# Second block's mixer rewritten: token-major queries and keys, twelve softmax units between recurrence levels and projections, eight bias transfers issued at once

## The chip, the core and the metric

The kernel runs on one NeuronCore of a Trainium2 chip. TensorE (PE) multiplies, VectorE (DVE) and ScalarE (ACT) work elementwise, GpSimd (POOL) issues some DMAs, SyncE (SP) issues the rest, and 16 DMA engines carry the data. Each engine runs its own list of instructions in order; semaphores tie the lists together. The metric is the device time of one execution in microseconds (us); less is better.

## The reference, cut to what is computed

256 tokens of width 1024 in fp32 pass through two equal hybrid layers (convolution, pooling and windowed attention with a distance bias, then a gated feed-forward part) and then through one other layer, the second block. The change is almost wholly in that block's mixer:

```python
h = rmsnorm(x, norm1_g) * (1 + sc1) + sh1                      # sc1, sh1 from c through w_ada
hq, hf, hi, hgt, nq, kc, vc, ks, vs, kw, vw, ng = split(h @ w_in)   # 4 x 512, 512, 6 x 128, 24 columns
# recurrence: 4 heads of 128, forget gate from hf
logf = log(lb + (1 - lb) * sigmoid(hf)); k = (1 - lb) * sigmoid(-hf); q = silu(hq); v = hi
S_t = exp(logf_t) * S_(t-1) + k_t v_t;  o_t = q_t S_t          # in all 256 tokens
o_hg = rmsnorm(o, norm_g) * silu(hgt)
# sparse attention: 8 query heads of 64, 2 key/value heads, first 16 dims of a head rotated
q, k_c, k_s, k_w = rope(rmsnorm(...) * gain)
k_cmp, v_cmp = silu((blocks of 32 tokens, stride 16, + pe) @ w1) @ w2       # 15 blocks
o_cmp = softmax(q k_cmp, masked) v_cmp
o_slc = softmax(q k_s over chosen blocks, causal) v_s          # 16 may be chosen, there are 4: all
o_win = softmax(q k_w, window 512, causal) v_w                 # the window is longer than the text
o_nsa = sigmoid(ng)[0] * o_cmp + sigmoid(ng)[1] * o_slc + sigmoid(ng)[2] * o_win
x = x + gt1 * (concat(o_hg, o_nsa) @ w_out)
x = x + gt2 * (feed-forward with a short causal convolution)
```

## The kernel before, in words

**Products.** Every fp32 value is held as two parts that fp32r can multiply: ACT makes the high one (L941), DVE the low one (L1237), and a product of the kernel is three matmuls (`product`, L587, L588, L589). Weights come as chunks of 1 MB through a ring of four slots on SP's queue. A chunk is split in two halves by ACT and DVE; chunk c+2 is split once the job that reads chunk c is over. Chunks of the compression weights (`c1k`, `c1v`) stay unsplit and are read as plain fp32.

**Jobs.** A job reads one chunk. `project` gives results with output columns on the partitions and 256 tokens in the free dimension: 48 products with 256 moving columns. `project_rows` gives them with tokens on the partitions: half of the contraction against 512 columns, 24 products with 512 moving columns, and two such jobs fill two banks. `project_tokens` is the same for up to 256 columns. Jobs 0 to 14 of the second block are `hf`, `hq`, `nq` (two each), `kc`, `ks`, `kw`, `vc`, `vv`, `ng` (the 24 branch gates, weights from the parameters), `hi`, `hg` (two each), and behind them four `out` jobs and the feed-forward part (`fa`, `fv`, `down`). `kc`, `ks`, `kw`, `vc` carry each head's columns twice, so that both halves of the partitions hold them.

**The recurrence.** It is computed as a 256 x 256 matrix of decayed products of queries and keys, by doubling levels: 0, then block sizes 1 to 64 (`LEVELS`), and a last one that joins the halves, nine in all. A level on PE is `level` (L761, 16 matmuls of 128 x 128, fp32, the last 8); DVE prepares its operands (`level_operands`, L1539 to L1550) between two exponentials on ACT (`level_exps`, L1086 to L1093) and copies its result out under a mask (`level_read_`, L1514, L1517). A table `HG_AT` puts levels behind certain jobs between `hq` 1 and `hi` 1.

**Behind the projections**, once the last level is read, stand one after the other: output of the recurrence (L776 to L778), mean squares of queries and keys and of the recurrence by matmuls with small picking tables (L783), their spreading over partitions (L799), a rotation matrix (L807), hidden layer of the compression (L823: each weight load is 30 columns of gathered blocks `Z`, and 256 weight columns move, 64 records in the trace for keys and values), its turning (L830), second weights (L837, L841), and eight softmax units: a unit is a pair of heads and half of the tokens, with two attention branches of up to 256 keys per head and the compressed one of 15. A unit goes scores (L860, L864) - `softmax2_in` on DVE (masked reads L1230, maximum) - exponentials on ACT (L1163) - `softmax2_out` on DVE (reciprocal, gates, scaling) - transposes (`turn2`, L876, L878) - copies on ACT (L1185, L1186) - values (L889 to L893). Then the four `out` jobs.

**The bias table.** At the program's start POOL writes the bias by distance to DRAM (L530) and reads it back skewed in eight transfers of 384 KB, two in flight: from the third on each waits for the one two before it (`bias_in`, L536). DVE's first masked read of the first layer's attention (L1230) waits for all eight.

## Time and profile before

| | us |
|---|---|
| median of 3 runs (1529.12 to 1537.22) | 1531.45 |
| the profiled execution, whole | 1538.83 |
| its span in the trace | 1537.0 |
| PE busy | 1430.1 |
| DVE busy | 1038.5 |
| ACT busy | 721.2 |
| POOL busy | 36.1 |
| mean granted clock of PE, share of full | 0.952 |

All numbers below come from the one profiled execution; its span begins with the first instruction and ends with the last. A busy PE need not be a PE at full speed: matmuls overlap, and the granted clock (PEclk) changes in the course of the span. A line number is that of kernel.py of the version shown (L587); "split", "h", "feed", "arena" and "psum" are names of tiles, where "h" is the normed input of the projections and "feed" the concatenated output of the mixer.

### The profile page before, as it was taken

The numbers are of one execution on the slowest core, as the hardware profiler recorded it, in microseconds if no ns is written. First come the engines' busy times: TensorE is split into PE (matmuls) and PEld (weight loads), VectorE is DVE, ScalarE is ACT, GpSimd is POOL, SyncE is SP. The second block draws the span as 40 slices with busy tenths as digits, with TensorE's granted clock in tenths as the row PEclk, the third lists the DMA queues.
The fourth block names the chain that finished last, engine by engine and source line by source line (L and its number), as shares of the span: only waits on it lengthen the run. The fifth ranks groups of instructions, "written<-read, shape, count | busy, mean of one in ns | idle before, by whom it ended". The sixth has DMA issues, their size and how long they took to land.

```text
span 1537.0 us, 25011 instructions
## 1 busy us (share of the span) xinstructions
PE 1430.1 (93%) x10188; PEld 1312.7 (85%) x10188; DVE 1038.5 (68%) x1679; ACT 721.2 (47%) x1128; POOL 36.1 (2%) x69
## 2 busy tenths in 40 slices
PE   7789998999999989999999999997999868899996
PEld 7679997988999989999989899996899445789995
DVE  4287677677677655876867767767665663677776
ACT  5244657444333444466563543335644163544452
POOL 0000000000000000000000000000000000000000
PEclk9889999999999999999999999998998876999998
DMA  9954544466767744544434576773442040445550
GB/s 273 208 183 155 175 165 138 145 203 216 254 230 256 252 145 140 169 161 162 140 133 169 204 259 240 246 258 117 141 165 86 4 161 1 135 170 175 192 192 28
DMA packets 41999, 262.98 MB, mean 171 GB/s; under 512 B 5195, under 2 KB 5451, under 8 KB 14372
## 3 DMA queue, kind: packets, MB, share of 16 engines
q1 hardware_dynamic: 32976, 229.66, 44.7%
q0 software_dynamic: 8784, 31.60, 6.1%
q8 instruction: 80, 1.31, 0.3%
q10 hardware_dynamic: 132, 0.18, 0.0%
q14 instruction: 27, 0.22, 0.0%
HBM read 259.85 MB, written 1.58 MB: 170 GB/s over the span
## 4 chain that ended last, share of the span: by engine, by line
PE 78%; DVE 11%; ACT 5%; DMA 5%; issue 2%; ACTq 0%; SPq 0%; POOL 0%; DVEq 0%
PE psum L587 23%; PE psum L588 23%; PE psum L589 23%; DMA arena<-bias_by_distance 4%; DVE split L1237 3%; DVE arena L1230 1%; ACT split L941 1%; PE psum L581 1%; PE psum L823 1%; PE psum L761 1%; PE psum L697 1%; PE psum L674 1%; DVE arena L1379 1%; PE psum L687 1%; ACT arena L958 1%
## 5 line engine op out<-in xcount | busy, mean ns | idle before, releaser
L587 PE MATMUL psum<-h,split 128*128 128x256 f32 x2304 | 662.3, 287 | 13.6 <-DVE split L1237 11.6
L588 PE MATMUL psum<-h,split 128*128 128x256 f32 x2304 | 656.3, 285 | 0.0
L589 PE MATMUL psum<-h,split 128*128 128x256 f32 x2304 | 656.0, 285 | 0.0
L1237 DVE TENSOR_TENSOR split<-ring,split 128x1024 fp32r<-128x1024 f32 x424 | 499.9, 1220 | 226.9 <-ACT split L941 226.2
L941 ACT CAST split<-ring 128x1024 fp32r<-128x1024 f32 x424 | 422.9, 1048 | 267.8 <-PE psum L589 255.6
L587 PEld LDWEIGHTS psum<-h,split 128*128 128x128 f32 x2304 | 446.5, 194 | 28.4 <-issue 16.7
L588 PEld LDWEIGHTS psum<-h,split 128*128 128x128 f32 x2304 | 446.8, 194 | 1.0
L589 PEld LDWEIGHTS psum<-h,split 128*128 128x128 f32 x2304 | 446.4, 194 | 0.0
L587 PE MATMUL psum<-split,feed 128*128 128x512 f32 x296 | 117.6, 397 | 5.6 <-DVE feed L1237 4.1
L588 PE MATMUL psum<-split,feed 128*128 128x512 f32 x296 | 117.1, 396 | 0.0
L589 PE MATMUL psum<-split,feed 128*128 128x512 f32 x296 | 116.5, 393 | 0.0
L587 PE MATMUL psum<-feed,split 128*128 128x256 f32 x288 | 84.0, 292 | 0.0
L589 PE MATMUL psum<-feed,split 128*128 128x256 f32 x288 | 82.5, 287 | 0.0
L588 PE MATMUL psum<-feed,split 128*128 128x256 f32 x288 | 82.5, 287 | 0.0
L1004 ACT ACTIVATE arena<-arena,small 128x256 f32<-128x256 f32 x64 | 32.1, 502 | 106.0 <-DVE small L1319 106.0
L1039 ACT ACTIVATE sig<-psum 128x512 f32<-128x512 f32 x46 | 27.5, 597 | 110.1 <-PE psum L589 110.0
L587 PEld LDWEIGHTS psum<-split,feed 128*128 128x128 f32 x296 | 56.7, 192 | 17.7 <-DVE feed L1237 4.6
L589 PEld LDWEIGHTS psum<-split,feed 128*128 128x128 f32 x296 | 56.6, 191 | 12.1
L588 PEld LDWEIGHTS psum<-split,feed 128*128 128x128 f32 x296 | 56.7, 192 | 10.7
L587 PEld LDWEIGHTS psum<-feed,split 128*128 128x128 f32 x288 | 56.4, 196 | 3.4 <-issue 3.4
L1451 DVE SCALAR_TENSOR_TENSOR arena<-arena 128x1024 f32<-128x1024 f32 x48 | 58.4, 1218 | 0.0
L588 PEld LDWEIGHTS psum<-feed,split 128*128 128x128 f32 x288 | 56.3, 196 | 0.0
(247 smaller groups left out, 1482.1 us busy)
## 6 DMA issues: line engine op xcount, KB each, us to landing
ring<-stream SPq DMA_DIRECT2D x215, 1024.0 KB, 4.9
arena<-ada POOLq DMA_DIRECT2D x48, 512.0 KB, 5.2
arena<-bias_by_distance POOLq DMA_DIRECT2D x8, 384.0 KB, 13.5
x<-x_in SPq DMA_DIRECT2D x2, 512.0 KB, 4.5
ring<-stream SPq DMA_DIRECT2D x2, 512.0 KB, 7.7
gain<-mod_rows POOLq DMA_DIRECT2D x2, 512.0 KB, 4.1
out<-x SPq DMA_DIRECT2D x4, 256.0 KB, 2.0
bias_by_distance<-arena POOLq DMA_DIRECT2D x1, 512.0 KB, 8.9
```

Source lines behind the costliest of these rows:

```text
L581: mm = pe.transpose(bank[(b0 + kt) % 8][:, i * P:(i + 1) * P], xs[:, i, kt * P:(kt + 1) * P], ident)
L587: pe.matmul(out_, a[0], b[0], start=first, stop=False)
L588: pe.matmul(out_, a[0], b[1], start=False, stop=False)
L589: return pe.matmul(out_, a[1], b[0], start=False, stop=last)
L674: mm = pe.matmul(bank[4 + hh][:, 0:T], qT[hh * HD:(hh + 1) * HD, p, n * P:(n + 1) * P], kd[hh * HD:(hh + 1) * HD, p // 2, :], start=True, ...
L687: mm = pe.transpose(bank[6][:, (2 * hh + s) * P:(2 * hh + s + 1) * P], S1[:, i % 2, hh, s * P:(s + 1) * P], ident)
L697: mm = pe.matmul(bank[7][hh * HD:(hh + 1) * HD, 0:T], v1[:, s, p // 2 * HD:(p // 2 + 1) * HD], PT[:, hh, s, :], start=(s == 0), stop=(s == 1))
L941: act.copy(split[:, c % 2, 0, n], ring[:, c % RING, n]).then_inc(wh_ready, 1)
L1004: act.activation(S1[:, i % 2, hh, :], S1[:, i % 2, hh, :], ACT.Exp, bias=nm[:, i % 2, hh:hh + 1], accum_out=rs[:, i % 2, hh:hh + 1])
L1039: act.activation(sig[:, i % 4], src, ACT.Sigmoid) \
L1237: return dve.tensor_tensor(out_, value, high.bitcast(F32), ALU.subtract)
L1451: dve.scalar_tensor_tensor(w, w, 1.0, c_row, ALU.mult, ALU.mult, accum_out=mod_l[:, a:a + 1]) \
```

## The change

Line numbers of after differ: L587 to L589 are L612 to L614, L761 is L786, L1237 is L1356, L1230 is L1349.

- **Order of chunks and jobs.** `nq`, `kk` (new: the two compression, selection and window keys and the compression values in one token-major job pair) come first, by rows; then `hf`, `hq`, `vv`, `ng`; the compression weights `c1k`, `c1v` come ahead of `hi` and `hg`, which are now by rows, too. `kc`, `ks`, `kw`, `vc` are gone: 13 projection chunks in place of 15. `out` is read in the order of quarters 0, 2, 1, 3: first both column halves of the recurrence's rows, last those of the attention's.
- **Norm and rotation token-major.** Squares on ACT (two), sums and root per token and head, scaling from PSUM on DVE; the rotation multiplies only the 16 rotated dims with tables that hold the gains (`rows_in`). Then 20 transposes (`turn_q`, `turn_k`) and copies on ACT with a gain per partition (`g_cols`). The picking, spreading and rotation matmuls and their tables are gone.
- **Hidden layer turned.** The weights are loaded, 128 columns at a time, and the 30 gathered blocks move: 128 records of 30 columns in place of 64 of 256, with no transposes behind them.
- **Compressed softmax once**, for all heads and tokens, in a few DVE instructions and one exponential.
- **Twelve units of 512 columns** (`unit2`): the first half of the tokens in units of two head pairs with 128 keys, the second half with one and 256 keys. `step(u)` issues scores of u+2, values of u-1 and transposes of u, and the steps stand between levels, `hg`, the recurrence's output and the `out` jobs.
- **The recurrence's output** is token-major, too, and is normed on DVE and transposed (`turn_hg`). The gate is kept token-major.
- **Zeroing** of six tiles goes to GpSimd, once the block's first norm has its input (`zeroed`); before, DVE zeroed two.
- **Bias.** The eight transfers are issued without waits between, on one semaphore.

```diff
@@ jobs and chunks
-    [("hf", 0), ("hf", 1), ("hq", 0), ("hq", 1), ("nq", 0), ("nq", 1),
-     ("kc", 0), ("ks", 0), ("kw", 0), ("vc", 0), ("vv", 0),
-     ("hi", 0), ("hi", 1), ("hg", 0), ("hg", 1)]
+    [("nq", 0), ("nq", 1), ("kk", 0), ("kk", 1), ("hf", 0), ("hf", 1), ("hq", 0), ("hq", 1), ("vv", 0)]
     + [("c1k", 0), ("c1k", 1), ("c1v", 0), ("c1v", 1)]
+    + [("hi", 0), ("hi", 1), ("hg", 0), ("hg", 1)]
     + [("out", j) for j in range(4)]
-HG_AT = {BJ["hq", 1] + a: i for i, a in enumerate((0, 1, 3, 4, 5, 7, 8, 10, 11))}
@@ POOL
-            for i, q0 in enumerate(range(0, P, SHIFTS)):
-                if i >= 2:
-                    pool.wait_ge(bias_in[i % 2], 16 * (i // 2))
+            for q0 in range(0, P, SHIFTS):
...
+            pool.wait_ge(x_ready, 8 * L + 4)
+            for a in (AT, hkh, SC, hid4, V4, kcmp):
+                pool.memset(a, 0.0).then_inc(zeroed, 1)
@@ PE, the order
+            h_in = each_of(h_ready, L * 16)
+            rows("nq", 0, h, 0, (0, 1), h_in)
+            rows("nq", 1, h, 1, (0, 1), h_in)
+            rows("kk", 0, h, 0, (2, 3))
+            rows("kk", 1, h, 1, (2, 3))
+            columns_of("hf", 0, 4)
+            turn_q()
+            columns_of("hf", 1, 5)
+            columns_of("hq", 0, 7)
+            turn_k()
...
+            level(0)
+            hidden(0)
+            level(1)
+            hidden(1)
+            level(2)
...
+            second_weights()
+            level(3)
+            score_compressed()
+            pe.wait_ge(*release2(("ng", 0)))
+            rows("hi", 0, h, 0, (4, 5))
+            scores2(0)
+            scores2(1)
+            rows("hi", 1, h, 1, (4, 5))
+            level(4)
+            turn_compressed()
+            pe.wait_ge(*release2(("hi", 1)))
+            rows("hg", 0, h, 0, (4, 5))
+            step(0)
+            level(5)
+            rows("hg", 1, h, 1, (4, 5))
+            step(1)
+            level(6)
+            step(2)
+            level(7)
+            step(3)
+            level(8)
+            hg_output()
+            step(4)
+            step(5)
+            pe.wait_ge(hg_read, 1)
+            turn_hg()
+            step(6)
+            pe.wait_ge(hmix_ready, 2)
+            rows("out", 0, feed, 0, (4, 5))
+            step(7)
+            rows("out", 1, feed, 0, (6, 7))
+            for u in range(8, UNITS2):
+                step(u)
+            values2(UNITS2 - 1)
+            mixed = {4 + 2 * p: (mix_ready, p + 1) for p in range(2)}
+            rows("out", 2, feed, 1, (4, 5), mixed)
+            rows("out", 3, feed, 1, (6, 7))
@@ new functions
+            def step(u):
+                if u + 2 < UNITS2:
+                    scores2(u + 2)
+                if u >= 1:
+                    values2(u - 1)
+                turn2(u)
...
+            def softmax2_out(u):
+                n, hh, ps = unit2(u)
+                groups = 2 * len(ps)
+                width = 4 * P // groups
+                dve.wait_ge(exp2, u + 1)
...
+                for g in range(groups):
+                    a = S2[u % 2][:, g * width:(g + 1) * width]
+                    ins = dve.tensor_scalar(a, a, rec[:, g:g + 1], None, ALU.mult)
                 ins.then_inc(p2_ready, 1)
@@ ACT, from level 5's exponentials on
+            level_exps(5)
+            split_high(15, L)
+            act.wait_ge(cmp_in, 1)
+            act.activation(cmp_p, cmp_p, ACT.Exp).then_inc(cmp_exp, 1)
+            exps2(0)
+            job_wait("hi", 1)
+            for i in range(NT):
+                e = act.copy(hv[:, i, :], bank[4 + i])
+            e.then_inc(act_evac, 1)
+            split_high(16, L)
+            exps2(1)
+            level_exps(6)
+            act.wait_ge(cmp_turned, 1)
```

PE, where the recurrence begins. Before, behind the product of the last job ahead of it (`hq` 1), level 0 and then a projection:

```order
L589 MATMUL psum<-h,split 128x256
L761 MATMUL psum<-arena 128x128 [waits hops_ready]
L761 MATMUL psum<-arena 128x128 x7
L587 MATMUL psum<-h,split 128x256 [waits wl_ready,act_evac]
L588 MATMUL psum<-h,split 128x256
L589 MATMUL psum<-h,split 128x256
```

After, behind `vv`, levels 0 and 1 with the hidden layer of the compression (L825; "ring" is the unsplit weight) between them:

```order
L614 MATMUL psum<-split,h 128x256
L786 MATMUL psum<-arena 128x128 [waits hops_ready]
L786 MATMUL psum<-arena 128x128 x7
L825 MATMUL psum<-arena,ring 128x30 [waits w_loaded1,z_ready]
L825 MATMUL psum<-arena,ring 128x30 x7
L825 MATMUL psum<-arena,ring 128x30 [waits w_loaded2]
L825 MATMUL psum<-arena,ring 128x30 x23
L786 MATMUL psum<-arena 128x128 [waits level_read,hops_ready]
L786 MATMUL psum<-arena 128x128 x7
L825 MATMUL psum<-arena,ring 128x30 [waits w_loaded3,z_ready]
```

The first levels had whole projections between them; now they have 64 small fp32 products each, with 30 moving columns.

DVE, the last levels of the recurrence before. L1514 and L1517 are the masked read and the copy of a level's result, L1237 the low half of a weight chunk, the others operands of a level:

```order
L1544 TENSOR_TENSOR arena<-arena 128x8x64 [waits hexp_q,level_done]
L1548 TENSOR_TENSOR arena<-arena 128x8x64 [waits hdiff]
L1550 TENSOR_TENSOR arena<-arena 128x8x64 [waits hexp_k]
L1514 COPY_PREDICATED arena<-pair_mask,psum 128x1024 [waits level_done,hcum_ready,hops_ready]
L1237 TENSOR_TENSOR split<-ring,split 128x1024 [waits wh_ready] x2
L1539 TENSOR_TENSOR arena<-arena 128x4x128
L1544 TENSOR_TENSOR arena<-arena 128x4x128 [waits hexp_q,level_done]
L1550 TENSOR_TENSOR arena<-arena 128x4x128 [waits hexp_k]
L1514 COPY_PREDICATED arena<-pair_mask,psum 128x1024 [waits level_done,hops_ready]
```

After, between the operands of one level and the read of the level before it stand a unit's scaling (L1771 to L1777) and the next unit's masked read and maximum (L1349, L1762, L1763):

```order
L1651 TENSOR_TENSOR arena<-arena 128x16x32
L1656 TENSOR_TENSOR arena<-arena 128x16x32 [waits hexp_q,level_done]
L1660 TENSOR_TENSOR arena<-arena 128x16x32 [waits hdiff]
L1662 TENSOR_TENSOR arena<-arena 128x16x32 [waits hexp_k]
L1771 RECIPROCAL arena<-arena 128x4 [waits exp2,hcum_ready,hops_ready]
L1774 TENSOR_TENSOR arena<-arena 128x4 [waits dve_step]
L1777 TENSOR_SCALAR sig<-sig,arena 128x128 [waits dve_step]
L1777 TENSOR_SCALAR sig<-sig,arena 128x128 x3
L1349 SCALAR_TENSOR_TENSOR sig<-psum,cst 128x512 [waits pt2_done,s2_done]
L1762 TENSOR_REDUCE arena<-sig 128x2 [waits s2_read]
L1763 TENSOR_SCALAR arena<-arena 128x2 [waits dve_step]
L1639 COPY_PREDICATED arena<-pair_mask,psum 128x1024 [waits level_done]
```

The softmax of the attention, which stood wholly behind the recurrence on DVE, has moved into its levels.

POOL at the program's start, before and after:

```order
L536 DMA arena<-bias_by_distance 16x16x384 [waits bias_out]
L536 DMA arena<-bias_by_distance 16x16x384
L536 DMA arena<-bias_by_distance 16x16x384 [waits bias_in0]
L536 DMA arena<-bias_by_distance 16x16x384 [waits bias_in1]
L536 DMA arena<-bias_by_distance 16x16x384 [waits bias_in0]
L536 DMA arena<-bias_by_distance 16x16x384 [waits bias_in1]
```

```order
L554 DMA bias_by_distance<-arena 256x1x512 [waits bias_sb]
L558 DMA arena<-bias_by_distance 16x16x384 [waits bias_out]
L558 DMA arena<-bias_by_distance 16x16x384 x7
L562 DMA arena<-c_in 128x1024 [waits bias_in]
L563 DMA pos_sb<-positions 128x2x1
L566 DMA rows_sb<-rows_in 128x384
```

The waits between the transfers are gone, and what follows them waits for one semaphore in place of two.

## Rows read from the trace of the kernel before

**Rows 1.** The page: its head, and the chain that ended last, by engine.
```profile
span 1537.0 us, 25011 instructions
...
PE 78%; DVE 11%; ACT 5%; DMA 5%; issue 2%; ACTq 0%; SPq 0%; POOL 0%; DVEq 0%
```

**Rows 2.** Windows, mixer's stages: us, busy (x count) each, PEclk, DMA share, GB/s.
```profile
1067.60:1148.00 80.40, 76.26 (x610) 74.83 (x610) 56.46 (x86) 44.82 (x59) 0.57 (x1) 0.97 0.43 147
1148.00:1187.00 39.00, 39.00 (x294) 39.00 (x294) 21.04 (x24) 19.82 (x26) 0.00 (x0) 0.87 0.27 91
1187.00:1239.00 52.00, 41.15 (x177) 22.54 (x177) 28.05 (x46) 10.18 (x16) 0.00 (x0) 0.87 0.18 65
1239.00:1277.00 38.00, 25.75 (x184) 18.36 (x184) 34.39 (x115) 28.54 (x109) 0.00 (x0) 0.77 0.21 82
1277.00:1321.05 44.05, 41.46 (x152) 27.98 (x152) 15.55 (x35) 14.36 (x33) 0.00 (x0) 0.73 0.16 51
```

**Rows 3.** Timeline of DVE, first layer's attention: start, us, instruction, [idle before it].
```profile
78.48 0.69 DVE L1230 SCALAR_TENSOR_TENSOR arena<-psum,arena 128x512 f32<-128x512 f32 x1 [21.77 <-DMA arena<-bias_by_distance]
```

**Rows 4.** Timeline of PE, a job by rows and one by columns.
```profile
1049.85 0.39 PE L588 MATMUL psum<-split,feed 128*128 128x512 f32 x1
1050.08 0.39 PE L589 MATMUL psum<-split,feed 128*128 128x512 f32 x1
...
1164.82 0.28 PE L589 MATMUL psum<-split,h 128*128 128x256 f32 x1
1164.94 0.28 PE L587 MATMUL psum<-split,h 128*128 128x256 f32 x1
```

**Rows 5.** Chain of waits in order of time, 1150 to 1200: start, us, what.
```profile
1155.72 3.61 PE psum L761 x16
...
1165.82 1.78 PE psum L761 x16
```

**Rows 6.** Groups by line and shape: busy, mean ns of one, idle before.
```profile
L1237 DVE TENSOR_TENSOR split<-ring,split 128x1024 fp32r<-128x1024 f32 x424 | 499.9, 1220 | 226.9 <-ACT split L941 226.2
...
L1316 DVE TENSOR_REDUCE small<-arena 128x2 f32<-128x512 f32 x32 | 22.0, 686 | 1.1
...
L1327 DVE TENSOR_SCALAR arena<-arena,small 128x256 f32<-128x256 f32 x64 | 19.7, 350 | 1.1
...
L1163 ACT ACTIVATE arena<-arena 128x256 f32<-128x256 f32 x16 | 7.9, 492 | 0.0
```

**Rows 7.** Waits of PE, 1064 to 1110: us in total, times, longest.
```profile
PE psum L587 <- DVE split L1237: 3.6, 2, 3.4
```

**Rows 8.** Timeline of PE, the hidden layer.
```profile
1218.71 15.77 PE L823 MATMUL psum<-ring,arena 128*30 128x256 f32 x64 [5.76 <-DVE arena L1596]
```

**Rows 9.** Windows about the branch gates (1147.9 to 1155.6); columns as in rows 2.
```profile
1148.00:1150.00 2.00, 2.00 (x21) 2.00 (x20) 0.64 (x2) 1.85 (x4) 0.00 (x0) 1.00 0.43 180
1152.00:1154.00 2.00, 2.00 (x11) 2.00 (x10) 2.00 (x3) 0.96 (x1) 0.00 (x0) 0.50 0.00 0
...
1162.00:1166.00 4.00, 4.00 (x36) 4.00 (x36) 0.66 (x1) 0.14 (x1) 0.00 (x0) 1.00 0.02 4
```

**Rows 10.** Timeline of ACT behind the branch gates.
```profile
1155.76 0.21 ACT L1117 ACTIVATE arena<-psum 128x48 f32<-128x48 f32 x1 [2.79 <-PE psum L589]
1155.98 1.28 ACT L1091 ACT_TABLE_LOAD   x1
```

**Rows 11.** Timeline of POOL, last two transfers of the bias table.
```profile
58.45 0.56 POOL L536 DMA_DIRECT2D arena<-bias_by_distance  x1 [6.46 <-DMA arena<-bias_by_distance]
64.78 0.56 POOL L536 DMA_DIRECT2D arena<-bias_by_distance  x1 [5.77 <-DMA arena<-bias_by_distance]
```

**Rows 12.** Windows of the first layer's start; columns as in rows 2.
```profile
20.00:72.00 52.00, 46.40 (x355) 44.81 (x354) 14.17 (x12) 17.66 (x21) 3.38 (x6) 0.93 1.01 233
72.00:76.00 4.00, 0.00 (x0) 0.00 (x0) 0.00 (x0) 0.00 (x0) 0.00 (x0) 0.93 0.75 96
...
80.00:84.00 4.00, 0.45 (x4) 0.00 (x0) 1.30 (x4) 3.60 (x9) 1.07 (x3) 0.50 0.80 178
```

1070 lines of the change are left out of this document (608 added, 462 removed), and 2 rows, old and new, of the table BLOCK2_JOBS.

## The prediction

> **What bounds the kernel now.** I read the page first: the chain that ended last runs 78% of the span over TensorE (PE), 11% over VectorE (DVE) [rows 1]. So I looked for the stages in which PE is not streaming weight products, by windows. The mixer of the second block reaches from its first projection at 1067.6 us to the first read of its last output bank at 1321.05 us, 253.4 us. Its five stages [rows 2] read: projections with recurrence levels (80.4 and 39.0 us, PE full), then normalising, rotating and compressing (52.0 us, PE busy 41 but loading weights only 22.5, DVE 28), then the softmax units (38.0 us, DVE 34 of 38 busy, ScalarE (ACT) 28.5), then the last values and four output projections (44.1 us, DVE and ACT a third busy, clock 0.73). The last three stages, 134 us, hold four projections, some 22 us of work; the rest is small work in a chain between three engines that covers none of the others. A second such place is the start: DVE waits 21.8 us for the bias table and goes on at 78.48 [rows 3].
>
> **Unit costs.** A projection by columns is 48 products of 256 columns, started every 0.12 us, so 5.8 us; one by rows is 24 products of 512 columns every 0.227 us, so 5.4 us [rows 4]. A recurrence level is 16 records in 1.78 us at full clock and 3.61 at half [rows 5], so 0.11 a record of 128 columns. One chunk costs DVE 2 x 1.2 us of splitting [rows 6] and ACT a little less, both under PE's 5.4. For a softmax unit of 512 columns DVE needs a masked read 0.69 [rows 3], a maximum 0.69, a few tiny ones, and scalings of 0.35 per 256 columns [rows 6]: 1.6 us before the exponentials, 1.05 to 1.3 behind them. ACT needs 0.5 per 256 columns [rows 6] and I take 0.6 for the copy of a turned tile of 512.
>
> **The change part by part.** I walk the new program in PE's order from 1067.6 on, and at each wait ask whether ACT or DVE, in their own order, is later.
>
> *A, up to the values' projection.* Eleven projections before the gates become nine: the duplicated keys and values go. Four by rows 21.8, five by columns 28.8, twenty transposes of 0.11 us 2.2; waits 3.4, the value that the same place (second chunk to third, ACT held by table loads) shows before [rows 7]; tables for the rotation are 16 wide where they were 256, so the wait hardly grows. Sum 56.2. The scaling and rotation in token order (about 2 x 6 us of DVE) lie under products of 5.4 us each; if they slipped PE would stand, at most by those 12.
>
> *B, from level 0 up to the gates of the recurrence.* PE runs level 0, hidden layer 0, level 1, hidden 1, level 2, branch gates, level 3, compressed scores, the `hi` projection in two halves with two score units, level 4. The hidden layer is turned round: before, 30 columns of weights and 256 moving, 64 records in 15.8 us [rows 8]; now 128 columns of weights and 30 moving, 128 records. No row has this form. The nearest is the branch gates' product, 24 columns moving: 21 records in 2 us at clock 1.00, then 11 in 2 us at 0.50, and the clock came back only in the projection behind the next level [rows 5, 9]. So a hidden layer costs 64 x 0.11 = 7.0 if the clock holds, 13.6 if it is half throughout. I take half soon after the start, since the gates did so: 11.0 and 10.5, gates 7.6, three levels of 3.5, level 0 and level 4 at 1.8, scores and second weights 5.3, `hi` 11.7, score units 1.8. Sum 62.0. Level 4 then ends late, and behind it stand, one after the other: DVE's operands 5 and the compressed softmax (3.6, PE waits), and transposes 0.5. B is 66.1; with the clock held, 48.
>
> *C, from there until the normalised recurrence is split.* `hg` needs banks 4 and 5, whose copy stands on ACT behind the exponentials of unit 0: wait 3.8. Then `hg` 0 5.4; scores, unit 0 turned and level 5 4.3 (the copy of compressed weights is behind `exps(6)`); `hg` 1 5.4; units 1 to 3 with levels 6 to 8 22.1, where DVE goes level operands 1.9, scale 1.05, mask and maximum 1.6, predicated copy 1.3, split 2.3 in a row, 7.4 a level; recurrence output 4.8; units 4 and 5 5.0; root and scaling 5.0, transposed and split 4.8. C is 60.6. Table switches on ACT (sigmoid, exponential, root, exponential) cost 1.28 us each [rows 10] and are in it.
>
> [...] In this trace the load begins at 1155.98, right behind an activation of 0.21 us begun at 1155.76, and is over in 1.28. [...]
>
> *D, to the end.* Output projection 5.5, unit 7 2.7, projection 5.4, units 8 to 11 13.2 (3.6 each: mask, exponentials, scale do not overlap on DVE), the last two projections 10.9. D is 37.7.
>
> A to D are 220.6 us. To that come handoffs: PE's last product ends 0.28 after its start where the walk counts 0.12 to 0.23, and a semaphore takes 0.05 to 0.15: 26 of them on the path, 6.5 us. And the clock: the small products of C and D, some 37 us, two thirds of them on the path, would run at the 0.77 that the softmax stage had [rows 2], 25 x 0.3 = 7.5. Together 234.6 against 253.4: **19 us** less. The output adds and the norm behind them stay as they are, and so does the feed-forward part.
>
> *The zeroing on GpSimd* (six memsets, before two on DVE): its start falls with the norm, whose tensors it doesn't share. No row shows a GpSimd memset of that size; I take 0, and at most 2 us if the norm is held back.
>
> *Bias unpaced.* Before, two of the eight transfers are in flight; each is issued when an older one lands, 6.3 us after the issue before it [rows 11]. From 20 to 72 us the 16 DMA engines are 1.01 busy, so nothing stood idle that eight transfers in flight could use; only in 72 to 76 the share is 0.75 at 96 GB/s [rows 12]. So the table comes at most some 3 us sooner if the queues share as before. If eight waiting transfers take a larger share from the weight ring, the table may be there by 60 to 65. PE stands from 71 us on only; what could then go is 7.4 us of standing before the table and some 5.6 behind it, while the first softmax runs (PE 0.45 of 4 us busy from 80 to 84 [rows 12]), 13 in all. Ends 0 and 13; I take 3, since the share of 1.01 is the nearest row. [...]
>
> **Sum.** 19 + 3 = 22 us. The profiled execution took 1538.8 (span 1537.0 [rows 1] and 1.8 around it), so 1516.8; the median of the runs is 1531.45, 7.4 lower, and gives 1509.5.
>
> **The rivals.**
> *The clock holds in B.* For: thirty columns in two records are more than 24 in one, and levels lie between. Against: the gates' row. DVE then becomes the later one in part, and of 18 us 15 come: 1494.5.
> *The bias comes early.* Larger share for the queue: 10 more, 1499.5.
> *The order on ACT and DVE binds in C and D.* ACT copies each turned tile only behind exponentials, splits and level exponentials, and DVE stands in softmax_in for scores that PE hasn't begun. One further handover of 1.2 us (a mask and maximum that start late) in each of twelve units: +14, 1523.5. For: DVE has 34 of 38 us busy in the old softmax stage. Against: a unit has fewer instructions now.
> *Slower: the clock stays half through C and D.* The tail before shows 0.73 over 44 us, with projections in it. If small products between any two projections keep it down, the six projections (32.6) and 25 us of small work take double: +50 beyond what is in the sum, 1559.5. It ends on the other side from 22 us on, that is with not quite half of it. Against: projections of one after another were at 1.00 again a few us after the drop [rows 9].
> *The change doesn't do what it says:* in D the units stand between nothing but themselves, since all out projections but two come before or after; this is in the sum already, with 13 us, and has no chance of its own.
>
> **How the numbers follow.** Forecast 0.42, clock holds 0.20, bias early 0.12, order binds 0.15, slower 0.11. Differences under 0.5%, 7.7 us, can't be told from no change here. The first three are all faster by more; the fourth, 8 us faster, lies at the border and is counted mostly as the same. Faster 0.78, same 0.12, slower 0.10. The range reaches from the clock held with the bias somewhat early, 1488, to order binding with the memset's 2 us and late handovers, 1529.
>
> **What would show it.** Right: from first projection to last output read 230 to 240 us; hidden layer records 0.21 us apart; PE stands once before the compressed transposes and once before `hg`, 3 to 4 us each; the bias' last landing at 74 to 78. Wrong: hidden records 0.11 apart (second case); DVE going on before 70 (third); units of D over 4.5 us (fourth); clock under 0.6 in the output projections (fifth); or weight products that wait for the ring, which I have nowhere.

## The result, and the profile after

The changed kernel takes 1513.6 us (median of 4 runs, 1509.4 to 1514.2) against 1531.2 before, a ratio of 0.987 with a 95% interval of 0.984 to 0.991: 17.5 us less. Run again among the experiments it took 1514.8 against 1529.7 (0.990, 0.987 to 0.994), 15.0 less. The forecast was 22 less, 1509.5. Both intervals are clear of no change, and both gains are smaller than the forecast.

The two profiled executions lie further apart, 24.6 us of span, and this splits in three. First, the start: the second block's first product begins at 1056.23 in place of 1067.64, 11.4 earlier. Second, the mixer, from there to the first multiplication of its last output bank: 241.0 us in place of 253.4 [rows 2], 12.4 less. Third, the rest, 0.7 less. The page's head, the instruction that ends the wait for the bias table (DVE timeline) and the eight transfers (POOL timeline), which answer to [rows 1, 3, 11]:

```profile
span 1512.4 us, 24473 instructions
```

```profile
69.55 0.69 DVE L1349 SCALAR_TENSOR_TENSOR arena<-psum,arena 128x512 f32<-128x512 f32 x1 [12.08 <-issue]
```

```profile
17.52 4.47 POOL L558 DMA_DIRECT2D arena<-bias_by_distance  x8 [8.49 <-DMA bias_by_distance<-arena]
69.75 0.57 POOL L562 DMA_DIRECT2D arena<-c_in  x1 [47.75 <-DMA arena<-bias_by_distance]
```

DVE goes on at 69.55, 8.9 us sooner than before, with all eight transfers in the queue from 22 us on.

The mixer, cut as the prediction's parts A to D, one row for each (windows; columns as in rows 2):

```profile
1056.20:1113.80 57.60, 55.37 (x357) 50.38 (x358) 46.36 (x118) 39.49 (x59) 0.56 (x1) 0.96 0.43 156
1113.80:1184.20 70.40, 66.82 (x354) 63.97 (x352) 25.80 (x43) 16.69 (x28) 0.00 (x0) 0.68 0.23 90
1184.20:1252.90 68.70, 52.42 (x266) 42.98 (x266) 48.05 (x99) 33.73 (x81) 0.00 (x0) 0.77 0.17 62
1252.90:1297.20 44.30, 40.13 (x193) 31.45 (x192) 20.33 (x41) 16.43 (x33) 0.00 (x0) 0.90 0.17 56
```

In B PE is busy 67 of 70 us and granted 0.68 of its clock. Its pieces there (timeline of PE): each half of the hidden layer is 32 products, which the trace shows as 64 records, and each level is 8 products in 16 records.

```profile
1113.79 1.95 PE L786 MATMUL psum<-arena 128*128 128x128 f32 x16
1115.58 11.12 PE L825 MATMUL psum<-arena,ring 128*128 128x30 f32 x64
1126.51 3.76 PE L786 MATMUL psum<-arena 128*128 128x128 f32 x16
1130.07 13.70 PE L825 MATMUL psum<-arena,ring 128*128 128x30 f32 x64
1143.58 3.76 PE L786 MATMUL psum<-arena 128*128 128x128 f32 x16
```

The windows of the second hidden layer and of the gates:

```profile
1130.10:1143.60 13.50, 13.50 (x66) 13.50 (x65) 3.76 (x5) 2.76 (x4) 0.00 (x0) 0.50 0.41 157
...
1147.10:1157.30 10.20, 10.20 (x51) 10.20 (x49) 8.87 (x12) 0.73 (x1) 0.00 (x0) 0.50 0.66 258
```

PE has no pause there, and the granted clock is 0.50 from 1118.8, inside the first hidden layer, to the end of the gates at 1157.3. The longest of what PE waits for in B to D (us in total, times, longest; L888 multiplies the values and waits for ACT's copies of the turned tiles, L914 turns the recurrence's output, L853 is the turning of the compressed scores, L612 a product, here the first of `hg`):

```profile
PE psum L888 <- ACT sig L1186: 6.9, 5, 3.2
PE psum L914 <- DVE arena L1886: 5.1, 1, 5.1
PE psum L853 <- DVE arena L1749: 3.6, 1, 3.6
PE psum L786 <- DVE arena L1639: 3.4, 2, 2.1
PE psum L612 <- ACT arena L1260: 3.2, 1, 3.2
```

### The profile page after: what moved, and what is told of

Same layout as the page of the kernel before. It is cut to its first block and busy times, and to the rows that moved or that the text cites. A ratio compares the mean times of both kernels' runs of the same rounds, so it can differ in the third digit from the quotient of the medians.

```text
span 1512.4 us, 24473 instructions
## 1 busy us (share of the span) xinstructions
PE 1415.6 (94%) x9942; PEld 1313.2 (87%) x9942; DVE 1023.3 (68%) x1670; ACT 709.9 (47%) x1090; POOL 40.1 (3%) x76
## 5 line engine op out<-in xcount | busy, mean ns | idle before, releaser
L1356 DVE TENSOR_TENSOR split<-ring,split 128x1024 fp32r<-128x1024 f32 x420 | 495.3, 1220 | 222.2 <-ACT split L1003 221.8
L612 PE MATMUL psum<-h,split 128*128 128x256 f32 x2176 | 622.0, 286 | 10.0 <-DVE split L1356 8.0
L613 PE MATMUL psum<-h,split 128*128 128x256 f32 x2176 | 617.2, 284 | 0.0
L614 PE MATMUL psum<-h,split 128*128 128x256 f32 x2176 | 617.2, 284 | 0.0
L1003 ACT CAST split<-ring 128x1024 fp32r<-128x1024 f32 x420 | 418.7, 1047 | 280.0 <-PE psum L614 267.5
L612 PEld LDWEIGHTS psum<-h,split 128*128 128x128 f32 x2176 | 419.1, 193 | 23.1 <-issue 15.3
L613 PEld LDWEIGHTS psum<-h,split 128*128 128x128 f32 x2176 | 419.0, 193 | 1.1
L614 PEld LDWEIGHTS psum<-h,split 128*128 128x128 f32 x2176 | 418.9, 193 | 0.0
L612 PE MATMUL psum<-split,feed 128*128 128x512 f32 x296 | 117.6, 397 | 5.6 <-DVE feed L1356 4.1
L614 PE MATMUL psum<-split,feed 128*128 128x512 f32 x296 | 115.9, 392 | 0.0
L612 PE MATMUL psum<-feed,split 128*128 128x256 f32 x288 | 84.0, 292 | 0.0
L614 PE MATMUL psum<-feed,split 128*128 128x256 f32 x288 | 82.5, 287 | 0.0
L612 PEld LDWEIGHTS psum<-split,feed 128*128 128x128 f32 x296 | 56.4, 191 | 17.5 <-DVE feed L1356 4.6
L612 PE MATMUL psum<-split,h 128*128 128x512 f32 (+1 forms) x176 | 66.3, 376 | 5.5 <-ACT arena L1260 3.2
L614 PEld LDWEIGHTS psum<-split,feed 128*128 128x128 f32 x296 | 56.4, 191 | 12.1
L613 PEld LDWEIGHTS psum<-split,feed 128*128 128x128 f32 x296 | 56.5, 191 | 10.5
L613 PE MATMUL psum<-split,h 128*128 128x512 f32 (+1 forms) x176 | 65.3, 371 | 0.0
L614 PE MATMUL psum<-split,h 128*128 128x512 f32 (+1 forms) x176 | 65.1, 370 | 0.0
```

The lines of the kernel that those rows point to most:

```text
L612: pe.matmul(out_, a[0], b[0], start=first, stop=False)
L613: pe.matmul(out_, a[0], b[1], start=False, stop=False)
L614: return pe.matmul(out_, a[1], b[0], start=False, stop=last)
L1003: act.copy(split[:, c % 2, 0, n], ring[:, c % RING, n]).then_inc(wh_ready, 1)
L1356: return dve.tensor_tensor(out_, value, high.bitcast(F32), ALU.subtract)
```

## The experiments

Every run was profiled and timed beside the kernel before. Runs 1 to 4 shared one chip and its runs of before (median 1529.7), and so did runs 5 to 8 (1530.5) and 9 to 11 (1527.1); run 12 had a fourth (1528.7). Across these groups only ratios can be compared, and the intervals of two ratios often overlap where the medians differ by 2 to 6 us. "Mixer" is the stretch defined above, read from the timelines of the one profiled execution; "table" is the start of the first masked read of the first layer's attention.

| run | median us | ratio to before (95%) | table | mixer |
|---|---|---|---|---|
| before | 1531.2 | | 78.5 | 253.4 |
| 1 changed kernel again | 1514.8 | 0.990 (0.987 to 0.994) | 71.2 | 239.4 |
| 2 before, bias unpaced | 1526.6 | 0.998 (0.996 to 1.001) | 73.8 | 249.8 |
| 3 changed, bias paced | 1521.1 | 0.994 (0.991 to 0.996) | 76.1 | 239.3 |
| 4 level 4 early | 1502.4 | 0.983 (0.980 to 0.986) | 70.3 | 226.4 |
| 5 hidden layer the old way | 1496.7 | 0.977 (0.974 to 0.980) | 69.5 | 222.0 |
| 6 hidden layer wide | 1496.6 | 0.978 (0.974 to 0.982) | 70.4 | 218.1 |
| 7 level 4, three exchanges | 1500.5 | 0.980 (0.977 to 0.983) | 72.2 | 221.8 |
| 8 as 7, hidden the old way | 1482.3 | 0.969 (0.965 to 0.972) | 71.9 | 206.7 |
| 9 before, gates wide | 1522.0 | 0.997 (0.994 to 1.000) | 77.9 | 240.4 |
| 10 as 7, hidden and gates wide | 1486.8 | 0.972 (0.968 to 0.976) | 69.9 | 212.5 |
| 11 as 8, gates wide | 1488.1 | 0.973 (0.969 to 0.976) | 70.6 | 212.4 |
| 12 as 11, copies between | 1484.9 | 0.971 (0.969 to 0.974) | 71.0 | 207.1 |

**Runs 1 to 3: what is the bias, what the mixer?** The theory was that the early table is real and worth half of the change, the rival that most of the difference between the two profiles is scatter. Run 2 takes the waits out of the kernel before, run 3 puts them into the changed one:

```diff
-            for q0 in range(0, P, SHIFTS):
+            for i, q0 in enumerate(range(0, P, SHIFTS)):
+                if i >= 2:
+                    pool.wait_ge(bias_in[i % 2], 16 * (i // 2))
```

> The changed kernel once more, beside the others on the same chip, as the yardstick for them. Both theories on the bias expect 16 to 19 us less than before, as measured, with the first masked read of the first layer's attention at 69 to 71 us.

> The kernel before with one part of the change alone: the eight bias transfers issued at once. Theory: the table lands near 69.5 us in place of 78.5, because eight waiting transfers take a larger share from the weight ring, and PE, which stood from 71 us on, goes through: 7 to 12 us less than before, half or more of the whole change. Rival (my forecast): queues share as before, the 9 us between the two profiles are scatter of the profiled execution of before, which was 7 us above its median: 0 to 4 us less.

> The changed kernel with the bias transfers paced again, two in flight: the mixer alone. Theory: table at 78 us, 7 to 12 us more than the changed kernel, so the mixer alone is worth only 7 to 10 us against before. Rival: 0 to 4 us more, the mixer is worth 14 to 18.

In the kernel before, taking the waits out gives 3.2 us by medians (the interval of run 2 just includes none); in the changed kernel, putting them back costs 6.3, with single runs that hardly overlap (1511.1 to 1518.3 in 6, 1514.7 to 1523.2 in 11). So neither theory held whole: the table does come earlier, at 70 to 74 us in every unpaced profile and at 76 to 78.5 in every paced one, but this is worth 3 to 6 us. The 11.4 us by which the second block began earlier in the first pair of profiles were too much: in run 9, whose start is the old one, the table came at 77.9 and the second block began at 1062.12; in the profile of before the table was 0.6 later and the second block 5.5 later. Runs 1 and 3 differ by 4.9 at the table (71.18 and 76.08) and by 4.9 at the second block (1057.43 and 1062.28). The mixer alone is then run 3 against before: 8.7 us less (interval 6 to 13). The single runs of the kernel before scatter by 12 us (1524.2 to 1536.7 in 22), and its profiled one (1538.8) is above all of them. The mixer of a single profile scatters too. From the first turned tile of the softmax (1252.6) to its end, a stretch that the edits of runs 2 and 9 do not touch, the same 300 records, with some 12 us of waits in each, took 68.4 us in the profile of before, 64.3 in run 2 and 58.7 in run 9, at granted clocks of 0.80, 0.87 and 0.97. The waits of PE from 50 to 110 us, first in run 1, then in run 3:

```profile
PE psum L699 <- ACT arena L1108: 7.1, 1, 7.1
PE psum L612 <- DVE split L1356: 3.7, 1, 3.7
```

```profile
PE psum L702 <- DVE arena L1352: 9.5, 1, 9.5
PE psum L615 <- DVE split L1359: 4.0, 1, 4.0
PE psum L702 <- ACT arena L1111: 1.8, 1, 1.8
```

Paced, PE stands 9.5 us for the table's reader (L1352) and 1.8 for the exponentials; unpaced, 7.1 for the exponentials alone, since the first softmax still stands there with too little beside it. 4.2 us go. The DMA queues show how the table gets there sooner. From 20 to 70 us the queue of the bias took 25.3% of the engines' time before and 26.7% in run 3 (2.8 MB each), and 28.9 to 30.3% in the first profile of the changed kernel, run 1 and run 2 (3.1 MB each); the queue of the weights took 75.1 and 74.3%, and 70.6 to 71.0%. The engines were as full as before, but the bias had a larger part of them.

**Run 4: a level that stood too late.** In the changed kernel DVE had the operands of level 4 ready at 1165.2, did the next half piece of work and then stood until PE reached that level behind the whole `hi` projection (DVE timeline):

```profile
1164.49 0.68 DVE L1662 TENSOR_TENSOR arena<-arena 128x512 f32<-128x512 f32 x1
...
1167.80 0.68 DVE L1651 TENSOR_TENSOR arena<-arena 128x512 f32<-128x512 f32 x1
1179.65 0.69 DVE L1656 TENSOR_TENSOR arena<-arena 128x512 f32<-128x512 f32 x1 [11.17 <-PE psum L786]
```

```diff
             rows("hi", 0, h, 0, (4, 5))
+            level(4)
             scores2(0)
             scores2(1)
             rows("hi", 1, h, 1, (4, 5))
-            level(4)
             turn_compressed()
```

> The changed kernel with the fourth recurrence level on PE ahead of the first scores and the second half of hi, its operands being there since 1165 us. Theory (the wait of 3.6 us before the compressed transposes and the one of 3.2 before hg are DVE and ACT standing still for 11 us for this level): both waits go, and the low clock that follows them in hg goes too; 5 to 9 us less than the changed kernel, hg 0 begins 6 us after turn_compressed's old place. Rival: DVE is the later engine further on anyway and the gain is given back at levels 6 to 8: under 2 us.

12.3 us less than run 1 by medians, 11.0 by ratios, more than the 5 to 9 expected. PE's wait before the compressed transposes is gone and that before `hg` is 0.7:

```profile
PE psum L888 <- ACT sig L1186: 5.3, 5, 1.8
PE psum L914 <- DVE arena L1886: 5.1, 1, 5.1
PE psum L786 <- DVE arena L1639: 3.9, 2, 2.2
PE psum L905 <- DVE arena L1642: 1.0, 1, 1.0
PE psum L612 <- ACT arena L1260: 0.7, 1, 0.7
```

These two waits gave 6.1 us of it. Behind the pause of the changed kernel `hg` 0 ran 8.5 us with a granted clock of 0.65; here it takes 5.7 at 1.00, 2.8 more. First the row of the changed kernel, then that of run 4:

```profile
1187.50:1196.00 8.50, 8.50 (x25) 6.51 (x25) 6.12 (x11) 5.00 (x13) 0.00 (x0) 0.65 0.53 181
```

```profile
1176.90:1182.60 5.70, 5.70 (x25) 4.46 (x25) 5.58 (x11) 3.92 (x12) 0.00 (x0) 1.00 0.57 187
```

Another 2.9 lie in this profile's first hidden layer, ahead of the edit, where the clock fell later (8.2 us at a mean clock of 0.88 in place of 11.1 at 0.63); that is not the edit's. So 8.9 us of the 12.3 are traced to the edit; for the rest the profiles name no one place.

**Runs 5 and 6: what brought the clock down?** Run 5 turns the hidden layer back (weights of 30 columns, 256 moving, and transposes behind levels 1 and 2), run 6 only repeats its 30 moving columns four times:

```diff
-                        mm = pe.matmul(hid_psum(kv)[:, m, :], ring[:, c % RING, at:at + P], Z[:, kv, r, :],
+                        mm = pe.matmul(bank[kv][:, 8 * NCMP * m:8 * NCMP * (m + 1)].rearrange("p (b a) -> p b a", b=4),
+                                       ring[:, c % RING, at:at + P],
+                                       Z[:, kv, r, :].unsqueeze(1).broadcast_to([P, 4, 2 * NCMP]),
...
```

> The changed kernel with the hidden layer of the compression the old way round: 30 columns of blocks as weights, 256 weight columns moving, 64 records, then two transposes for each of keys and values behind levels 1 and 2. In the changed kernel the layer runs 11.0 and 13.5 us, most of it at half clock, and levels 1 and 2 and the gates behind it are at half, too. Theory (128 products with 30 moving columns are what brings the clock down): the records start 0.25 us apart as before, 7.9 us each half, levels 1 and 2 take 1.8 to 2 us each, granted clock over 0.9 until the gates; 8 to 14 us less than the changed kernel. Rival (the clock falls here for any small work): 64 records at half clock are 0.43 us each, 27 us, and the kernel is 2 to 4 us slower than the changed one.

> The changed kernel with the hidden layer's 30 moving columns repeated four times, 120 in a product, the result read from the first 30. A level's product of 128 moving columns is started every 0.11 us at full clock, as a product of 30 is, so the repetition costs nothing at full clock. Theory (the granted clock follows how many columns the array works on): the clock stays at 1.00 longer, the two halves take 7.0 to 9 us in place of 11.0 and 13.5; 4 to 8 us less than the changed kernel. Rival (the clock follows something else, such as the type of the products, fp32 in two passes): the same 24.5 us in all and no difference, under 1 us.

Both are 18 us faster than run 1 by medians, 19 to 20 by ratios. Of run 5, 8 to 14 were expected, of run 6, 4 to 8: both theories had the direction and priced it too low. The single runs of run 6 fall in two groups of three, 1490.5 to 1492.8 and 1500.4 to 1504.4; its median lies between them, and its profile is of the lower group. Timeline of PE in run 6:

```profile
1113.26 1.95 PE L786 MATMUL psum<-arena 128*128 128x128 f32 x16
1115.05 7.30 PE L825 MATMUL psum<-arena,ring 128*128 128x120 f32 x64
1122.19 1.96 PE L786 MATMUL psum<-arena 128*128 128x128 f32 x16
1123.98 7.30 PE L825 MATMUL psum<-arena,ring 128*128 128x120 f32 x64
1131.12 1.96 PE L786 MATMUL psum<-arena 128*128 128x128 f32 x16
```

Against the first profile of the changed kernel, the same number of records with four times the columns takes 14.6 us in place of 24.8, and levels 1 and 2 go from 3.76 to 1.96 each: 13.8 us, at a granted clock of 1.00 where it was 0.63 in the first half and 0.50 behind it. The gates behind them, still 24 columns wide, run at full clock too and take 5.5 in place of 10.2, 4.7 more (window of run 6):

```profile
1132.80:1138.30 5.50, 5.50 (x52) 5.50 (x50) 5.15 (x9) 2.65 (x3) 0.00 (x0) 0.98 0.40 124
```

Behind these gates the clock did fall: from 1138.3 to 1145.0 it was 0.50, with PE busy all the time. Run 5 reads like run 6 in the hidden layer:

```profile
1110.10 1.95 PE L789 MATMUL psum<-arena 128*128 128x128 f32 x16
1111.97 7.09 PE L826 MATMUL psum<-ring,arena 128*30 128x256 f32 x32
1119.00 2.05 PE L789 MATMUL psum<-arena 128*128 128x128 f32 x16
1120.98 7.09 PE L826 MATMUL psum<-ring,arena 128*30 128x256 f32 x32
```

At a granted clock of 1.00 the records of 30 columns started every 0.11 us (19 of them in the 2.02 us from 1115.58 in the first profile), those of 120 every 0.11 too (64 in 7.1 us, run 6), and those of 256 every 0.22 (32 in 7.0 us, run 5). Run 5's rival takes 0.43 us for a record of 256 at half clock; in the kernel before, whose layer began at 0.50, eight of them took 3.1 us, about 0.4 each. The "two passes" of run 6's rival are the two records in which the traces show each fp32 product: 32 for the 16 products of a half in run 5, 64 for the 32 in run 6.

Over levels 0 to 2 and both halves the clock was 1.00 with run 5's 64 records of 256 columns and with run 6's 128 of 120, and 0.63 and 0.50 in the two halves with 128 of 30: this is the theory of run 5, as far as this place shows it. That the clock follows the columns as such, the theory of run 6, is not shown: its gates, 24 columns wide, ran at 0.98 and only the work behind them at 0.50.

So the layer turned round and made wide is as long as the old one (7.3 against 7.1 for each half); with 30 columns it lost 10 us, and the levels and gates behind it lost another 8. The rivals are out: the clock does not fall here for any small work (run 5), nor for fp32 records as such (run 6).

**Run 9: the same in the kernel before.** The gates' 24 columns are repeated ten times:

```diff
+                        if n == 24:
+                            out_ = bank[b][:, m * T:m * T + 240].rearrange("p (b a) -> p b a", b=10)
+                            w_ = [a.unsqueeze(1).broadcast_to([P, 10, 24]) for a in w_]
...
```

> The kernel before with one edit: the 24 moving columns of the branch gates repeated ten times, 240 in a product, the result read from the first 24. In its profile the gates take 7.7 us, the last two thirds at half clock, level 1 behind them 3.6, and the projection behind that begins at half. Theory (narrow products bring the clock down, whatever the code around them): gates 5.3 us, level 1.8 to 2, the projection at once at 0.12 a product; in all 4 to 7 us less than before. Rival (the clock of this place was to fall anyway, or 240 columns cost more than 24): same within 1 us, or 5 us more if a product takes 0.21.

5.1 us less by medians, within the 4 to 7 expected, though the interval of the ratio (0.994 to 1.000) reaches nearly to no change. The windows of the gates, level 1 and the projection behind it in run 9, which answer to [rows 5, 9]:

```profile
1142.60:1147.90 5.30, 5.30 (x50) 5.30 (x49) 3.99 (x5) 4.80 (x6) 0.00 (x0) 1.00 0.15 62
1147.90:1149.70 1.80, 1.80 (x19) 1.80 (x18) 1.80 (x3) 1.61 (x3) 0.00 (x0) 1.00 0.00 0
1149.70:1155.50 5.80, 5.80 (x50) 5.80 (x50) 3.59 (x5) 1.04 (x2) 0.00 (x0) 1.00 0.53 184
```

From the first product of the gates to the next level it is 12.8 us, where the kernel before took 17.8 (1147.9 to 1165.7): 5.0 less, which is what the medians show. The mixer of this profile is 9 to 13 us shorter than those of run 2 and before; 5.6 to 9.7 of that lie in the stretch at the end named above, far behind the gates, and are not counted as the edit's.

Runs 6 and 9 agree on repeating narrow columns: with it the clock was at 1.00 in the hidden layer and in the gates, where it had been 0.63 and 0.50 in the halves of the one (changed kernel) and 0.68 in the other (before, 1147.9 to 1155.6). No wait of PE was needed for the low clock: PE was busy 13.50 of 13.50 us and the clock was at 0.50 all the same.

**Runs 7 and 8: order on ACT and DVE, and the sum.** Three exchanges on top of run 4; the first of them, on ACT:

```diff
             level_exps(8)
+            copy_turned2(2)
             job_wait("hg", 1)
             for i in range(NT):
                 e = act.activation(hsg[:, i, :], bank[4 + i], ACT.Sigmoid)
             e.then_inc(act_evac, 1)
-            copy_turned2(2)
             exps2(4)
...
```

The gate's multiplication on DVE goes behind `level_read_(7)`, and the sums, the root and the scaling of the recurrence's norm ahead of unit 6's exponentials and scaling.

> On top of the early fourth level, three exchanges on ACT and DVE: the copy of unit 2's transposes ahead of the gate's sigmoid and its table loads, the gate's multiplication behind the read of level 7, and sum, root and scaling of the recurrence's norm ahead of unit 6's exponentials and scaling. Theory (the order on ACT and DVE binds in C): PE's waits of 1.6 to 3.2 us before unit 2's values and of 5.1 us before the recurrence's transposes shrink by 1 to 2 and 2 to 3 us; 3 to 5 us less than with the early level alone. Rival: the same work only waits one place later, under 1 us.

> The early fourth level, the three exchanges and the old hidden layer together. Theory: the gains add where they lie in different stretches: the sum of what the three show alone, 18 to 30 us less than the changed kernel. Rival: with PE faster in B, DVE and ACT (level operands, splits, compressed values) become the later engines there and a third or more of the hidden layer's gain is lost.

Run 7's mixer is 4.6 us shorter than run 4's, but 1.6 of this lies in part A, which the exchanges do not touch; the medians differ by only 1.9, less than the 3 to 5 expected, and the intervals overlap. A gain of the exchanges is likely and not proved. Its waits show part of the gain going one place on: before the recurrence's transposes 2.3 in place of 5.1, before the values 3.7 in place of 5.3, but before the recurrence's output 3.0 in place of 1.0 and 1.6 new before the first `out`:

```profile
PE psum L888 <- ACT sig L1186: 3.7, 4, 1.8
PE psum L905 <- DVE arena L1642: 3.0, 1, 3.0
PE psum L914 <- DVE arena L1885: 2.3, 1, 2.3
PE psum L612 <- DVE feed L1356: 1.6, 1, 1.6
```

Run 8 adds the old hidden layer: 1482.3 us, 48 less than before and some 32 less than the changed kernel. That is more than the 18 to 30 expected. The parts alone gave 12.3, 1.9 to 4.6 and 18, so 32 to 35 in all, against 32.5 by medians and 33.5 by ratios: they add.

**Runs 10 to 12: where it stops.** Wide gates on top, once with the wide hidden layer, once with the old one; then ACT's copies of the compression's second weights between level 4's two exponentials.

> Early fourth level, the three exchanges, the hidden layer's 30 columns repeated four times and the gates' 24 repeated ten times. Theory: with the clock at full from level 0 to the compressed scores the stretch of B falls by 14 to 18 us against the early level with the exchanges alone; 1480 to 1486 us. Rival: gates at full speed add nothing, because DVE's operands of levels 3 and 4 are then the later ones: within 2 us of the kernel with the old hidden layer (1482).

> The same with the hidden layer the old way round and the wide gates. Its sibling without wide gates had the gates at 0.65 and level 3 at 0.78 of the clock, some 12 us of half or nearly half clock. Theory: 3 to 5 us less than the sibling, 1477 to 1480 us, and the best of all. Rival: DVE (5.8 of 6 us busy there) is the later engine and nothing is gained.

> The kernel of run 11 (early level, exchanges, old hidden layer, wide gates) with ACT's six copies of the compression's second weights between the two exponentials of level 4 in place of behind them. In run 11 PE stood 2.0 us for them, and its clock fell to 0.61 behind the pause and gave the next 8 us at half. Theory (run 11 lost the gates' gain to this pause): the wait is under 0.7 us, the clock of the compressed scores and of hi stays over 0.85, 1477 to 1484 us, 4 to 9 less than run 11 (1488). Rival: the clock falls at these narrow products (30 and 64 columns) with or without the pause: within 2 us of run 11.

None of the three came out as its theory had it: 1480 to 1486, 1477 to 1480 and 1477 to 1484 us were expected, and 1486.8, 1488.1 and 1484.9 measured. Wide gates on top of run 8 (run 11) gave nothing: by medians run 11 is some 6 us slower, which neither of my two cases had, though the intervals of the two ratios overlap. Run 10 has no partner without wide gates and shows nothing of them by itself. In run 11 PE now reached the compressed scores before ACT's copies, waited 2.0 us (2.5 in run 10), and ran the next 5.4 at 0.57 (the next 8.0 at 0.57 as well):

```profile
1144.60:1146.50 1.90, 0.00 (x0) 0.00 (x0) 1.89 (x3) 1.84 (x7) 0.00 (x0) 1.00 1.01 427
1146.60:1152.00 5.40, 5.40 (x22) 4.88 (x23) 3.24 (x8) 0.90 (x2) 0.00 (x0) 0.57 0.52 217
```

With the copies between (run 12) the wait is 0.42 and the clock holds through the same work:

```profile
PE psum L858 <- ACT arena L1170: 0.4, 1, 0.4
```

```profile
1141.60:1149.00 7.40, 7.40 (x41) 6.44 (x42) 4.70 (x11) 1.86 (x3) 0.00 (x0) 1.00 0.60 248
```

Its mixer is 5.3 us shorter than run 11's, but 1.6 of this is again in part A; its median is 3.2 lower, and by ratios, over two chips, it is only 1.8. The wait and the clock went as the theory said, the time only in part.

This pause explains little of the difference between runs 8 and 11, though. From level 0 to the first `out` product run 8 took 108.5 us, run 11 109.6 and run 12 105.9. Behind it, to the end of the mixer, they took 40.6, 45.2 and 45.3, with a granted clock of 1.00, 0.88 and 0.88. So run 12 was 2.6 us ahead of run 8 at the first `out` and lost 4.7 in part D. The windows there, first of run 8, then two of run 12:

```profile
1233.00:1265.80 32.80, 28.90 (x157) 22.46 (x155) 16.63 (x33) 12.82 (x27) 0.00 (x0) 1.00 0.22 74
```

```profile
1218.00:1224.00 6.00, 6.00 (x17) 4.73 (x18) 2.87 (x8) 1.09 (x4) 0.00 (x0) 0.63 0.01 1
...
1248.00:1254.00 6.00, 6.00 (x21) 4.82 (x20) 0.69 (x1) 0.58 (x1) 0.00 (x0) 0.57 0.00 0
```

Part D is the same program in all three. Whether its clock is scatter from one execution to the next or follows from the pauses before it stays open; no run took those away.

## Why the prediction was right, and where it was off

**Right:** the direction, the range and the place. The median came 4 us above the forecast, inside 1488 to 1529. Some of this was luck: the range was 41 us wide, and two errors of opposite sign, in the mixer and in the bias, partly cancelled.

**Part A** was forecast at 56.2 and measured 57.6 in the first profile and 56.0 in run 1. The longest wait was 1.9 in place of 3.4. The 1.6 between the two profiles goes with the clock: 0.83 from 1070 to 1080 us in the first, 1.00 in the same work of run 1.

**Part B** held the term that was too small: 66.1 forecast, 70.4 measured. The mechanism and most sizes held: hidden 0 at 11.1 (11.0 forecast), level 1 at 3.76 (3.5), the wait before the compressed transposes 3.6 (3.6). But the clock stayed down to the end of the gates, where I had let it come back in parts: hidden 1 13.7 for 10.5, gates 10.2 for 7.6. Those two are 5.8 us. The choice between held and half clock was made rightly, by the gates' row; the step that failed was giving back a part of it with no row to say so. The rival "the clock holds" priced it at 15 us; by runs 5 and 6 it is 18.

**Parts C and D** were 98.3 in the walk, with 14.0 of handoffs and low clock on top for all the mixer; measured 113.0. The waits that the walk named are there: 3.2 before `hg` (3.8 forecast), 5.1 for root and scaling (5.0). Two sums in it were wrong. The five pieces of DVE's work for a level add up to 8.15 us and not 7.4, so that three levels are 24.5 and not 22.1; 24.7 were measured (1204.88 to 1229.61). And four units of 3.6 are 14.4 and not 13.2; 16.6 were measured (1267.98 to 1284.55). The largest sum of waits in the profile, 6.9 us in five waits for ACT's copies of turned tiles, has no term of its own; 3.2 of it stand before unit 2's values, behind the gate's sigmoid. The 0.05 to 0.15 us for a semaphore stand in no row; in the same trace DVE begins 0.02 us behind ACT's root (1196.28 to 1196.30) and PE 0.15 behind DVE's reciprocal (1198.04 to 1198.19). Of the low clock, 2.8 us came as `hg` 0 at 0.65, behind a pause, where I had set 7.5 aside for small products only.

**The mixer as a whole** was forecast to give 19 and gave 8.7 by medians (run 3), 12.4 in the pair of profiles. Of the gap of some 10 us, hidden 1 and the gates are 5.8. Another 3.6 or more is the yardstick: the profile of before, against which I summed, had a mixer of 253.4 where run 2 has 249.8, with the clock of its last stretch at 0.80 against 0.87. The sign that I gave for it, 230 to 240, was just missed in the first profile (241.0) and met in runs 1 and 3 (239.4 and 239.3). The records of the hidden layer were 0.21 us apart, as said, in its second half only; in the first, with the clock falling on the way, they were 0.17 apart on average.

**The bias** was taken at 3 of 0 to 13. It is worth 3.2 in the old kernel and 6.3 in the changed one. The sign given for the forecast, a last landing at 74 to 78, was missed by every unpaced profile of the changed kernel, in which DVE went on at 69.5 to 72.2. The sign of the second rival, DVE going on before 70, was just met in the first profile (69.55) and in runs 5 and 10, but its price of 13 was not paid back: the softmax chain behind the table still stands alone. The step that failed was taking the share of 1.01 to mean that more transfers in flight gain nothing: the engines did no more work, but the queue of the bias had 29 to 30% of them in place of 25 to 27. A gain near 0, the low end of what I gave, does not hold here: every unpaced profile has the table 2 to 9 us earlier than the paced ones. How the engines divide their time between the queues no run shows beyond these shares.

So the mixer's gain was forecast 7 to 10 us too high and the bias's 3 too low; of the 22 us in all, 15.0 to 17.5 came.

**The zeroing** on GpSimd shows no cost: six memsets take 3.29 us from 1045.8 on, inside the norm, for which PE stands 9.4 us in the changed kernel and in the one before alike. No run takes it away. **The order on ACT and DVE** was given 14 us at 0.15. It bound at one place I had walked past: level 4 behind `hi` 1. I wrote the order down, priced what stands behind it (5 and 3.6 us), and did not ask whether it could stand earlier; run 4 shows 12.3 us in it by medians. Of the late handovers that this rival did mean, run 7 shows 2 to 3 us, not proved. **The slower rival** did not come: the part with the output projections ran at 0.90.

## What to carry to other kernels

When an edit makes matmuls narrower, look for a row of the same width and price the edit at the clock of that row, and count the work behind it too: here the changed kernel's levels 1 and 2 (3.76 us each, 1.96 in run 6) and its gates (10.2 us, 5.5 in run 6) ran at 0.50 behind products of 30 columns, and in the kernel before the start of a projection (1159.3 to 1160.0) at 0.50 behind those of 24. Repeating a narrow moving operand cost nothing in the time of a product here (the gates took 5.5 us with 24 columns at a clock of 0.98 and 5.3 with 240 at 1.00) and gave 18 and 5 us in two kernels, the 5 with an interval of 0 to 10. Where the next thing behind it is a wait, as in run 11, it may give nothing. When one profile is the yardstick, look at the clock in the stretches that the edit leaves alone: here one such stretch took 58.7 to 68.4 us. And where an engine stands for 10 us behind one small instruction of another, look for the earliest place at which that instruction's operands are ready.

## What the runs showed of the hardware

- 64 fp32 records of 30 moving columns took 13.7 us at a clock of 0.50 (changed), 64 of 120 columns 7.3 at 1.00 (run 6); 48 fp32r products of 24 columns took 7.7 us at a clock of 0.68 (before), 10.2 at 0.50 (changed) and 5.5 at 0.98 (run 6); with 240 columns they took 5.3 at 1.00 (run 9). At 1.00 a record of 30 and one of 120 columns both started every 0.11 us, one of 256 every 0.22 (run 5). So between 30 and 120, and between 24 and 240, it is the clock that the width moved here, and not the time of a product at a given clock.
- The clock fell without any pause of PE (1.00 from 1115.6 to 1118.2, 0.50 from 1118.8, with PE busy 10.90 of 10.90 us and then 13.50 of 13.50), and it was also low behind pauses of 2.0 and 3.2 us (0.57 and 0.65). With the pause of 2.0 cut to 0.4 it stayed at 1.00 in the same work (run 12).
- In the kernel before (its own profile, runs 2 and 9), the same 300 records of PE at the end of the mixer, with some 12 us of waits in each, took 68.4, 64.3 and 58.7 us, at granted clocks of 0.80, 0.87 and 0.97.
- Eight transfers of 384 KB issued at once in one queue let their reader go on at 69.5 to 73.8 us, two at a time at 76.1 to 78.5, with the engines' share at 1.0 in both. From 20 to 70 us their queue had 29 to 30% of the engines' time at once, 25 to 27% two at a time.
